# Summing the first norm's squares on TensorE, and loading X and the first weights ahead of parameters and bias rows

## The chip, the cores and the metric

The kernel runs on one core of a Trainium2 chip. The metric is the device time in microseconds (us) of one execution; lower is better. A core has TensorE (matmuls, PE in the profile), VectorE (DVE), ScalarE (ACT), GpSimd (POOL) and SyncE (SP), each with its own instruction queue, and 16 DMA engines that all queues share.

## The reference

A trunk of two layers over X, 1024 tokens of 1024 features in float32. The change touches only the first layer's first norm:

```python
def rmsnorm(x, g):
    xf = x.astype(jnp.float32)
    y = xf * lax.rsqrt(jnp.mean(xf * xf, axis=-1, keepdims=True) + NORM_EPS)
    return (y * g.astype(jnp.float32)).astype(x.dtype)
...
for l in range(DEPTH):
    h = rmsnorm(x, mix_norm_gain[l])
    proj = h @ w_in[l]
...
    x = x + y @ w_out[l]
    x = x + conv_ffn(rmsnorm(x, ffn_norm_gain[l]), ...)
```

`proj` feeds three mixers (an SSD scan, a gated MLP, dilated attention); their concatenated result goes through `w_out`, and a convolutional FFN follows.

## The kernel before

**Layout.** X lies transposed in on-chip memory: 8 tiles (k) of 128 features by 1024 tokens. The tokens are worked in two halves (th = 0, 1) of 512. Every float32 product is made of three matmuls (`mm3`, or the three of `tokens_part`) of a high and a low part: HH and HL for the activations, WH and WL for the weights. GpSimd splits each weight unit, as it arrives in RAW, into WH and WL, two halves a unit; there are two slots, and a unit takes a slot when TensorE has begun the unit after it.

**Engines.** Each engine runs one program, written out by hand and tied to the others by semaphores. Nothing is reordered across waits on an engine. TensorE's first real work is `keys_unit`: for th = 0, then 1, and k = 0 to 7, it waits for h_ready of that k and runs 12 matmuls (four token tiles by three).

**The first norm before.** The squares i = 0 to 7 belong to th = 0, i = 8 to 15 to th = 1.
- ScalarE (`first_norm`, `squares`, line 962) waits for a quarter of X for each four squares and writes the square of one k: the first of each half into ACC, the others into four buffers SQ.
- VectorE (`total`, line 1325) adds each SQ buffer into ACC: 14 adds in all.
- TensorE (`norm_spread`, line 501) sums ACC over the 128 features with 4 small matmuls against a column of ones, once per half, into a PSUM bank (NB).
- VectorE (`mean`, lines 1329 and 1331) makes mean and reciprocal, ScalarE (`root`, line 966) the root, TensorE (`norm_back`, line 509) spreads the result over the partitions.
- For each k VectorE scales X (`scaled`, line 1340, into HF), ScalarE copies HF to HH (`high_norm`, line 972), VectorE subtracts (`low_norm`, line 1346, HL), which raises h_ready.

In `keys_unit` of layer 0 `norm_spread` of the second half stands ahead of k = 5 and `norm_back` ahead of k = 7. VectorE's adds of the second half stand between its tiles of the first.

**Transfers.** SyncE's queue: the constants CST (266 KB; identity, triangles, ones), then X in four quarters of 1 MB, with the first weight unit (two halves of 512 KB) ahead of the third quarter. ScalarE's queue: OH, TAB and ROW (the tables of the relative bias, needed by a small product behind `keys_unit`, line 614), then PARM (layer parameters, 847 KB), which waits for TensorE's first increments; VectorE waits for PARM ahead of the first `mean`.

Of the kernel before, what the change touches and what calls it, by code (L numbers as in the profile page):

```python
# [25 lines left out]
P = 128  # L26
DEPTH, SEQ, DM = 2, 1024, 1024
KT = DM // P
# [11 lines left out]
NG = FFN // UC  # L40
# [61 lines left out]
NB = (3, 7)  # L102
# [31 lines left out]
def trunk(nc, xT, wst, params, consts, onehot, lnrow, table, outT):  # L134
# [10 lines left out]
    with ExitStack() as ctx:  # L145
# [14 lines left out]
        PARM = place("PARM", [P, NPAR])  # L160
        CST = place("CST", [P, 4 * P + 20])
# [25 lines left out]
        TAB = place("TAB", [NBUCK, AH_], top[0])  # L187
        NACS = place("NACS", [P, NT, 16])
        QGN = place("QGN", [P, 1])
        ident, tri_f, tri_b, ones = (CST[:, i * P:(i + 1) * P] for i in range(4))  # L190
# [23 lines left out]
        ACC = place("ACC", [P, SEQ], u_at + 16384)  # L214
        SQ = place("SQ", [P, 4, HALF], u_at + 24576)
        HF = place("HF", [P, 4, HALF], u_at + 32768)
        ROW = place("ROW", [AH_, 2 * SEQ], u_at + 40992)
        OH = place("OH", [NBUCK, 2 * SEQ], u_at + 49184)
# [55 lines left out]
        PS = ctx.enter_context(nc.psum_tensor("PS", [P, 8, HALF], F32))  # L274

        def sem(name):
# [4 lines left out]
        cst_in, par_in, oh_in = sem("cst_in"), sem("par_in"), sem("oh_in")  # L281
# [3 lines left out]
        sq_ready, sq_used, ss_ready = sem("sq_ready"), sem("sq_used"), sem("ss_ready")  # L285
        inv_ready, rs_ready, nb_ready, ib_ready = sem("inv_ready"), sem("rs_ready"), sem("nb_ready"), sem("ib_ready")
# [38 lines left out]
        f_tap, f_conv, f_silu, f_hi, act_ready, f_step = (  # L325
            sem("f_tap"), sem("f_conv"), sem("f_silu"), sem("f_hi"), sem("act_ready"), sem("f_step"))
# [11 lines left out]
        def half(th):  # L338
            return slice(th * HALF, (th + 1) * HALF)
# [23 lines left out]
        def _(sp):  # L363
# [11 lines left out]
                    with sp.Fori(first, last) as u:  # L375
                        unit(u)

            sp.dma_start(CST[:], consts[:, :]).then_inc(cst_in, 16)
            for i in range(4):
                k, th = slice(i % 2 * 4, i % 2 * 4 + 4), i // 2  # L380
                if i == 2:
# [21 lines left out]
            for l in range(DEPTH):  # L403
# [43 lines left out]
                for part in range(2):  # L447
                    sp.wait_ge(yn_ready, l * NT + 6 + 2 * part)
                    sp.wait_ge(yt_full, 2 + l * NT + 6 + 2 * part)
                    k = slice(part * 4, part * 4 + 4)  # L450
# [29 lines left out]
        def _(pe):  # L480
# [15 lines left out]
            def norm_spread(n, th):  # L496

                pe.wait_ge(sq_used, n * SUMS + norm_done(n, th))
                for t in range(4):
                    a = th * HALF + t * P  # L500
                    last = nc.tensor.matmul(PS[:, NB[th], 2 * t:2 * t + 2], ACC[:, a:a + P], ones[:, 0:2],  # L501
                                            start=True, stop=True)
                last.then_inc(nb_ready, 1)

            def norm_back(n, th):

                pe.wait_ge(rs_ready, 2 * n + th + 1)
                for t in range(4):
                    last = nc.tensor.matmul(PS[:, NB[th], t * P:(t + 1) * P],  # L509
                                            IR[:, th, t:t + 1].to_broadcast((P, P)), ident, start=True, stop=True)  # L510
                last.then_inc(ib_ready, 1)
# [61 lines left out]
            def keys_unit(l, a0):  # L573

                n = 2 * l
                unit_ready(l, 0)
                if l:
                    pe.wait_ge(a_free, 4 + a0)
                for th in range(2):
                    for k in range(KT):  # L580
                        if th == 0 and k == (2 if n else 5):
                            norm_spread(n, 1)
                        if th == 0 and k == (5 if n else 7):
                            norm_back(n, 1)
                        pe.wait_ge(h_ready, (2 * n + th) * KT + k + 1)
                        for t in range(th * 4, th * 4 + 4):
                            if k == 0:
                                bank_ready(a0, t)
                            last = tokens_part(0, t, k, A_BANK[t], l > 0 and t == k == 0)
                            if k == KT - 1:  # L590
                                last.then_inc(a_full, 1)
# [11 lines left out]
            for l in range(DEPTH):  # L603
                a0, b0 = l * A_FILLS, l * B_FILLS
                if l == 0:
                    norm_spread(0, 0)
                    norm_back(0, 0)
                keys_unit(l, a0)
                if l == 0:
# [3 lines left out]
                    for q in range(4):  # L613
                        last = nc.tensor.matmul(PS[0:AH_, 4 + q, :], TAB[:, :], OH[:, q * HALF:(q + 1) * HALF],
                                                start=True, stop=True)
# [277 lines left out]
                n = 2 * l + 1  # L893
# [51 lines left out]
        def _(act):  # L945
            A = nc.scalar.activation

            def squares(n, b_value, first, end):

                for i in range(first, end):  # L950
                    dt, th = norm_order(n)[i]
                    if n:
                        act.wait_ge(b_free, b_value + i + 1)
                    else:
                        act.wait_ge(x_in[i // 4], 16)
                    to = ACC[:, half(th)]
                    if i in norm_sums(n):
                        j = norm_sums(n).index(i)
                        if j >= 4:
                            act.wait_ge(sq_used, n * SUMS + j - 3)  # L960
                        to = SQ[:, j % 4, :]
                    A(to, X[:, dt, half(th)], ACT.Square).then_inc(sq_ready, 1)
# [5 lines left out]
            def high_norm(n, th, first, end):  # L968
                for k in range(first, end):
                    i = (2 * n + th) * KT + k  # L970
                    act.wait_ge(hf_ready, i + 1)
                    A(HH[:, k, half(th)], HF[:, i % 4, :], ACT.Copy).then_inc(hh_ready, 1)
# [9 lines left out]
                      ).then_inc(vh_ready, 1)  # L982

            def first_norm():
                squares(0, 0, 0, 8)
                root(0, 0)
                high_norm(0, 0, 0, 4)
                squares(0, 0, 8, 13)
                high_norm(0, 0, 4, 5)
                squares(0, 0, 13, 15)  # L990
                high_norm(0, 0, 5, 6)
                squares(0, 0, 15, 16)
                root(0, 1)
                high_norm(0, 0, 6, KT)
                high_norm(0, 1, 0, 1)
                token_out(0, 0)
                high_norm(0, 1, 1, KT)
# [26 lines left out]
                root(n, 1)  # L1024
                high_norm(n, 1, 0, KT)

            act.dma_start(OH[:], onehot[:, :]).then_inc(oh_in, 16)
            act.dma_start(TAB[:], table[:, :]).then_inc(oh_in, 16)
            act.dma_start(ROW[:], lnrow[:, :]).then_inc(oh_in, 16)
            act.sem_inc(a_free, 4)  # L1030
            for l in range(DEPTH):
                a0, b0 = l * A_FILLS, l * B_FILLS
                act.wait_ge(act_ready, 1 + l * NG * 2)
                act.dma_start(PARM[:], params[l]).then_inc(par_in, 16)
                nc.scalar.preload_act_table(ACT.Sqrt)
                if l == 0:
                    first_norm()
# [153 lines left out]
                for i in range(NT):  # L1191
                    n, par = l * NT + i, i % 2
# [4 lines left out]
                    if i == 2:  # L1197
# [3 lines left out]
                        for h in range(4):  # L1201
                            last = A(MHL[:, :, h, :], PS[:, 6, 0:2 * P].rearrange("p (a n) -> p a n", a=2), ACT.Copy,
                                     scale=fourth[:, h:h + 1])
# [26 lines left out]
                for c in range(NT):  # L1230
                    n, par = l * NT + c, c % 2
# [7 lines left out]
                    for j in range(4):  # L1239
# [4 lines left out]
                        for h in range(4):  # L1244
                            e = d * 8 + g * 4 + h
                            last = A(SEG[par][:, j, h, :], PS[:, 2 + j % 2, h * P:(h + 1) * P], ACT.Exp,
                                     bias=NACS[:, c, e:e + 1])
# [5 lines left out]
                    for h in range(HEADS):  # L1253
                        cols = slice(h * HD, (h + 1) * HD)
                        last = A(Y2[:, cols], PS[:, 6, cols], ACT.Copy, scale=EACS[:, c, 8 + h:9 + h])
# [17 lines left out]
                for g in range(NG):  # L1273
                    n = l * NG + g
# [40 lines left out]
        def _(dve):  # L1315
            TT, STT, TS = nc.vector.tensor_tensor, nc.vector.scalar_tensor_tensor, nc.vector.tensor_scalar

            def total(n, i):

                th = norm_order(n)[i][1]  # L1320
                j = norm_sums(n).index(i)
                dve.wait_ge(sq_ready, n * 16 + i + 1)
                if j:
                    dve.wait_ge(sq_used, n * SUMS + j)
                TT(ACC[:, half(th)], ACC[:, half(th)], SQ[:, j % 4, :], ALU.add).then_inc(sq_used, 1)  # L1325
# [23 lines left out]
            def scale_on(n, th, first, end):  # L1349

                for k in range(first, end):
                    if k < KT:
                        scaled(n, th, k)
                    if k:
                        low_norm(n, th, k - 1)

            def first_norm():
                for i in range(1, 8):
                    total(0, i)
                dve.wait_ge(par_in, 16)  # L1360
                mean(0, 0)
                scale_on(0, 0, 0, 4)
                for i in range(9, 12):
                    total(0, i)
                scale_on(0, 0, 4, 5)
                for i in range(12, 14):
                    total(0, i)
                scale_on(0, 0, 5, 6)
                for i in range(14, 16):
                    total(0, i)  # L1370
                mean(0, 1)
                scale_on(0, 0, 6, KT + 1)
                scale_on(0, 1, 0, KT + 1)

            def mix_norm(n, add):
# [50 lines left out]
            for l in range(DEPTH):  # L1426
# [56 lines left out]
                for x in range(2):  # L1483
                    nc.vector.memset(PAD[:, x, 0:2], 0.0)
                    last = nc.vector.memset(PAD[:, x, SEQ + 2:SEQ + 4], 0.0)
# [451 lines left out]
```

## Time and profile before

| | |
|---|---|
| median of 3 runs | 2678.39 us (2677.86 to 2683.78) |
| the profiled execution | 2681.2 us, of it 2679.4 us span |
| TensorE busy | 2575.6 us (96%) |
| VectorE / ScalarE / GpSimd busy | 1482.6 / 896.7 / 730.8 us |
| mean granted TensorE clock | 0.988 of full |

Times in the trace count from the span's start. PE is TensorE's matmuls, PEld its weight loads, which overlap; a float32 matmul of tiles that are not split shows as two entries. PEclk is the granted clock as a share of 2.4 GHz. In a timeline row the bracket says how long the engine was idle before the instruction, and what released it.

### The profile page before, as it was taken

The page shows a single profiled execution, that of the slowest core. Times are in us where ns is not written, and L with a number is a line of the kernel's source. Part 1 is how long each engine was busy: PE and PEld are TensorE (multiplying, and loading weights), DVE is VectorE, ACT ScalarE, POOL GpSimd, SP SyncE. Part 2 cuts the span into 40 slices and gives each one's busy share as a digit, 9 for nine tenths or more (in the row PEclk, how much of TensorE's full clock was granted, in tenths as well). Part 3 has the DMA queues.
Part 4 walks back from the last instruction along what each step waited for, and adds up shares of the span by engine and source line. Part 5 has one row for each costly group of instructions (what it writes and reads, how often), then busy time and mean ns, then how long its engine had stood idle before and what let it go on. Part 6 is the DMA issues. An engine that isn't in the chain of part 4 may idle for free. (4 is left out here: it accounts for less than half of the span.)

```text
span 2679.4 us, 33472 instructions
## 1 busy us (share of the span) xinstructions
PE 2575.6 (96%) x13350; PEld 2177.3 (81%) x13350; DVE 1482.6 (55%) x1743; ACT 896.7 (33%) x1550; POOL 730.8 (27%) x388
## 2 busy tenths in 40 slices
PE   5999998899999999999999999988999999999998
PEld 5988986788888888888789889877888888888887
DVE  5376558837444444444575755696464444444445
ACT  3245556613222222222233465574132222222221
POOL 2332111024333333333323311100433333333331
PEclk8999999899999999999999999999999999999999
DMA  4443443121111111111123344521111111111111
GB/s 177 144 117 119 132 152 124 48 81 48 47 47 48 48 53 48 49 47 48 54 109 80 109 134 140 171 85 69 48 47 48 47 47 48 49 51 50 48 47 71
DMA packets 73725, 209.90 MB, mean 78 GB/s; under 512 B 5832, under 2 KB 28360, under 8 KB 72264
## 3 DMA queue, kind: packets, MB, share of 16 engines
q1 hardware_dynamic: 53384, 178.58, 20.3%
q10 hardware_dynamic: 20200, 29.30, 3.3%
q8 instruction: 106, 1.74, 0.3%
q14 instruction: 35, 0.29, 0.0%
HBM read 176.37 MB, written 31.49 MB: 78 GB/s over the span
## 5 line engine op out<-in xcount | busy, mean ns | idle before, releaser
L484 PE MATMUL PS<-HH,WH 128*128 128x512 f32 x1920 | 756.6, 394 | 4.9 <-issue 4.9
L474 POOL CAST WH<-RAW 128x1024 fp32r<-128x1024 f32 x192 | 238.7, 1243 | 1888.3 <-PE PS L484 1403.2
L488 PE MATMUL PS<-HH,WL 128*128 128x512 f32 x1920 | 753.3, 392 | 0.0
L487 PE MATMUL PS<-HL,WH 128*128 128x512 f32 x1920 | 753.2, 392 | 0.0
L476 POOL TENSOR_TENSOR WL<-RAW,WH 128x1024 fp32r<-128x1024 f32 x192 | 497.4, 2591 | 15.4
L1755 DVE TENSOR_TENSOR X<-PS,X 128x512 f32<-128x512 f32 x384 | 259.6, 689 | 378.7 <-PE PS L488 378.4
L484 PEld LDWEIGHTS PS<-HH,WH 128*128 128x128 f32 x1920 | 362.5, 189 | 84.3 <-issue 5.3
L488 PEld LDWEIGHTS PS<-HH,WL 128*128 128x128 f32 x1920 | 361.7, 188 | 81.3
L487 PEld LDWEIGHTS PS<-HL,WH 128*128 128x128 f32 x1920 | 362.2, 189 | 78.3
L1284 ACT ACTIVATE FPAD<-PS 128x512 f32<-128x512 f32 x176 | 102.6, 596 | 885.8 <-PE PS L488 885.8
L1773 DVE SCALAR_TENSOR_TENSOR CVV<-FPAD,PARM,CVV 128x1024 f32<-128x1024 f32 x44 | 95.3, 2166 | 377.8 <-ACT CVV L1290 377.8
L484 PE MATMUL PS<-AHI,WH 128*128 128x512 f32 x704 | 278.9, 396 | 4.9 <-DVE X L1755 4.9
L488 PE MATMUL PS<-AHI,WL 128*128 128x512 f32 x704 | 278.5, 396 | 0.0
L487 PE MATMUL PS<-ALO,WH 128*128 128x512 f32 x704 | 278.0, 395 | 0.0
L555 PE MATMUL PS<-WH,HH 128*128 128x256 f32 (+1 forms) x896 | 264.4, 295 | 12.7 <-DVE HL L1346 12.7
L558 PE MATMUL PS<-WL,HH 128*128 128x256 f32 (+1 forms) x896 | 256.9, 287 | 0.0
L559 PE MATMUL PS<-WH,HL 128*128 128x256 f32 (+1 forms) x896 | 256.9, 287 | 0.0
L555 PEld LDWEIGHTS PS<-WH,HH 128*128 128x128 f32 x896 | 174.1, 194 | 16.5 <-DVE HL L1346 9.0
L558 PEld LDWEIGHTS PS<-WL,HH 128*128 128x128 f32 x896 | 174.2, 194 | 0.1
L559 PEld LDWEIGHTS PS<-WH,HL 128*128 128x128 f32 x896 | 174.0, 194 | 0.0
L484 PEld LDWEIGHTS PS<-AHI,WH 128*128 128x128 f32 x704 | 133.1, 189 | 37.0 <-DVE X L1755 6.6
L488 PEld LDWEIGHTS PS<-AHI,WL 128*128 128x128 f32 x704 | 132.9, 189 | 31.3
(198 smaller groups left out, 3080.9 us busy)
## 6 DMA issues: line engine op xcount, KB each, us to landing
RAW<-wst SPq DMA_DIRECT2D x192, 512.0 KB, 3.5
TOE<-toe_d SPq DMA_DIRECT2D x64, 512.0 KB, 3.7
XBS<-xbc_d SPq DMA_DIRECT2D x24, 512.0 KB, 4.5
xspill<-X ACTq DMA_DIRECT2D x2, 4096.0 KB, 13.1
xbc_d<-CV ACTq DMA_DIRECT2D x16, 512.0 KB, 3.9
X<-xspill SPq DMA_DIRECT2D x4, 2048.0 KB, 7.3
tok_d<-ST ACTq DMA_DIRECT2D x12, 512.0 KB, 3.4
ZG<-tok_d SPq DMA_DIRECT2D x16, 384.0 KB, 3.6
```

Source lines behind the costliest of these rows:

```text
L474: nc.gpsimd.tensor_copy(hi, raw).then_inc(hi_done, 1)
L476: nc.gpsimd.tensor_tensor(lo, raw, hi.bitcast(F32), ALU.subtract).then_inc(w_ready, 1)
L484: ins = nc.tensor.matmul(out, wh, xh, start=first, stop=False)
L487: nc.tensor.matmul(out, wh, xl, start=False, stop=False)
L488: return nc.tensor.matmul(out, wl, xh, start=False, stop=last)
L555: ins = nc.tensor.matmul(o, xh, wh, start=(k == 0), stop=False)
L558: nc.tensor.matmul(o, xh, wl, start=False, stop=False)
L559: return nc.tensor.matmul(o, xl, wh, start=False, stop=(k == KT - 1))
L1284: A(FPAD[:, x % 2, 1 + th * HALF:1 + (th + 1) * HALF], bank(f % 4), ACT.Copy).then_inc(a_free, 1)
L1755: TT(x, bank(4 + i % 4), x, ALU.add).then_inc(b_free, 1)
L1773: step.then(STT(t, FPAD[:, x % 2, 0:SEQ], PARM[:, at:at + 1], t, ALU.mult, ALU.add))
```

## The change

- `first_norm` on VectorE loses all 14 `total`. In their place TensorE gets `square_sum(i)`: for each of the 16 squares, four matmuls of the kind of `norm_spread`, accumulated over k in the bank. Squares 0 to 7 are summed ahead of `norm_back(0, 0)`; squares 8 to 15 in pairs ahead of k = 1 to 4 of `keys_unit`. The `norm_spread` of both halves goes from the first norm. TensorE frees the SQ buffers.
- ScalarE's squares of the second half go in pairs between its copies of k = 0 to 3.
- CST moves from SyncE's queue to the front of ScalarE's. PARM of layer 0 is issued behind square 3, without a wait for TensorE, and OH, TAB and ROW behind square 7.

```diff
@@ sync
-            sp.dma_start(CST[:], consts[:, :]).then_inc(cst_in, 16)
             for i in range(4):
@@ tensor
+            def square_sum(i):
+
+                th, k = divmod(i, KT)
+                pe.wait_ge(sq_ready, i + 1)
+                square = SQ[:, (th * (KT - 1) + k - 1) % 4, :] if k else ACC[:, half(th)]
+                for t in range(4):
+                    last = nc.tensor.matmul(PS[:, NB[th], 2 * t:2 * t + 2], square[:, t * P:(t + 1) * P], ones[:, 0:2],
+                                            start=(k == t == 0), stop=(k == KT - 1), skip_group_check=True)
+                if k:
+                    last.then_inc(sq_used, 1)
+                if k == KT - 1:
+                    pe.wait_ge(sq_used, (th + 1) * (KT - 1))
+                    pe.sem_inc(nb_ready, 1)
@@ keys_unit
-                        if th == 0 and k == (2 if n else 5):
+                        if th == 0 and n and k == 2:
                             norm_spread(n, 1)
+                        if th == 0 and not n and 1 <= k < 5:
+                            square_sum(6 + 2 * k)
+                            square_sum(7 + 2 * k)
                         if th == 0 and k == (5 if n else 7):
                             norm_back(n, 1)
@@ layer 0
-                    norm_spread(0, 0)
+                    for i in range(KT):
+                        square_sum(i)
                     norm_back(0, 0)
@@ scalar, first_norm
-                squares(0, 0, 0, 8)
+                squares(0, 0, 0, 4)
+                act.dma_start(PARM[:], params[0]).then_inc(par_in, 16)
+                squares(0, 0, 4, 8)
+                act.dma_start(OH[:], onehot[:, :]).then_inc(oh_in, 16)
+                act.dma_start(TAB[:], table[:, :]).then_inc(oh_in, 16)
+                act.dma_start(ROW[:], lnrow[:, :]).then_inc(oh_in, 16)
                 root(0, 0)
-                high_norm(0, 0, 0, 4)
-                squares(0, 0, 8, 13)
-                high_norm(0, 0, 4, 5)
-                squares(0, 0, 13, 15)
-                high_norm(0, 0, 5, 6)
-                squares(0, 0, 15, 16)
+                for k in range(4):
+                    high_norm(0, 0, k, k + 1)
+                    squares(0, 0, 8 + 2 * k, 10 + 2 * k)
+                high_norm(0, 0, 4, 6)
                 root(0, 1)
@@ scalar, ahead of the layers
-            act.dma_start(OH[:], onehot[:, :]).then_inc(oh_in, 16)
-            act.dma_start(TAB[:], table[:, :]).then_inc(oh_in, 16)
-            act.dma_start(ROW[:], lnrow[:, :]).then_inc(oh_in, 16)
+            act.dma_start(CST[:], consts[:, :]).then_inc(cst_in, 16)
...
-                act.wait_ge(act_ready, 1 + l * NG * 2)
-                act.dma_start(PARM[:], params[l]).then_inc(par_in, 16)
+                if l:
+                    act.wait_ge(act_ready, 1 + l * NG * 2)
+                    act.dma_start(PARM[:], params[l]).then_inc(par_in, 16)
@@ vector, first_norm
-                for i in range(1, 8):
-                    total(0, i)
                 dve.wait_ge(par_in, 16)
                 mean(0, 0)
-                scale_on(0, 0, 0, 4)
-                for i in range(9, 12):
-                    total(0, i)
-                scale_on(0, 0, 4, 5)
-                for i in range(12, 14):
-                    total(0, i)
-                scale_on(0, 0, 5, 6)
-                for i in range(14, 16):
-                    total(0, i)
+                scale_on(0, 0, 0, 7)
                 mean(0, 1)
-                scale_on(0, 0, 6, KT + 1)
+                scale_on(0, 0, 7, KT + 1)
```

## Rows read from the trace of the kernel before

**Rows 1.** The page: the engines' shares, and the chain's engines.

```profile
PE 2575.6 (96%) x13350; PEld 2177.3 (81%) x13350; DVE 1482.6 (55%) x1743; ACT 896.7 (33%) x1550; POOL 730.8 (27%) x388
...
PE 30%; DVE 1%; issue 0%; ACT 0%; DVEq 0%
```

**Rows 2.** Waits of TensorE, whole span: us in total, times, longest.

```profile
PE PS L501 <- DVE ACC L1325: 21.9, 5, 17.3
...
PE PS L555 <- DVE HL L1346: 12.7, 8, 3.4
```

**Rows 3.** Timeline to 25 us, all engines: start, duration, engine and line.

```profile
6.67 0.36 ACTq L1034 DMA_DIRECT2D PARM<-par  x1
...
9.22 0.63 ACT L962 ACTIVATE ACC<-X 128x512 f32<-128x512 f32 x1 [0.87 <-DMA X<-xT]
...
12.91 2.19 ACT L962 ACTIVATE SQ<-X 128x512 f32<-128x512 f32 x4 [1.50 <-DMA X<-xT]
...
15.36 1.39 POOL L474 CAST WH<-RAW 128x1024 fp32r<-128x1024 f32 x1 [14.91 <-DMA RAW<-wst]
...
17.35 1.87 PE L501 MATMUL PS<-CST,ACC 128*128 128x2 f32 x8 [17.35 <-DVE ACC L1325]
...
19.99 2.07 PE L509 MATMUL PS<-CST,IR 128*128 128x128 f32 x8 [0.78 <-ACT IR L966]
...
22.10 1.40 DVE L1340 SCALAR_TENSOR_TENSOR HF<-X,PARM,PS 128x512 f32<-128x512 f32 x2 [2.40 <-PE PS L509]
...
25.00 0.55 PE L555 MATMUL PS<-WH,HH 128*128 128x256 f32 x1 [2.94 <-DVE HL L1346]
```

**Rows 4.** Transfers issued before 130 us: KB each, us to landing.

```profile
PARM<-par ACTq DMA_DIRECT2D x1, 847.0 KB, 7.9
...
OH<-onehot ACTq DMA_DIRECT2D x1, 256.0 KB
```

**Rows 5.** One microsecond by engine; last two columns DMA share and GB/s.

```profile
9.00:10.00 1.00, 0.00 (x0) 0.00 (x0) 0.00 (x0) 0.78 (x2) 0.00 (x0) 1.00 1.06 391
```

**Rows 6.** Line 501 alone in a stretch: PE busy, PEld busy, PEclk, DMA, GB/s.

```profile
590.00:600.00 10.00, 0.95 (x8) 1.05 (x8) 1.00 0.00 1
```

**Rows 7.** Timeline from 28 to 49 us, POOL's last row and TensorE's.

```profile
28.61 2.73 POOL L476 TENSOR_TENSOR WL<-RAW,WH 128x1024 fp32r<-128x1024 f32 x1
...
34.80 0.39 PE L555 MATMUL PS<-WH,HH 128*128 128x256 f32 x1 [3.37 <-DVE HL L1346]
...
40.19 1.70 PE L501 MATMUL PS<-CST,ACC 128*128 128x2 f32 x8
...
44.61 0.41 PE L558 MATMUL PS<-WL,HH 128*128 128x256 f32 x1
...
47.17 0.41 PE L558 MATMUL PS<-WL,HH 128*128 128x256 f32 x1
...
48.88 1.43 PE L509 MATMUL PS<-CST,IR 128*128 128x128 f32 x8
...
54.08 0.28 PE L555 MATMUL PS<-WH,HH 128*128 128x256 f32 x1
...
55.50 0.28 PE L555 MATMUL PS<-WH,HH 128*128 128x256 f32 x1
```

**Rows 8.** VectorE's lines before 64 us: count, busy us, mean ns, idle before.

```profile
L1325 DVE TENSOR_TENSOR ACC<-ACC,SQ 128x512 f32<-128x512 f32 x14 | 11.5, 821 | 13.2 <-ACT SQ L962 12.2
```

**Rows 9.** Busy us (count) of PE, PEld, DVE, ACT, POOL; PEclk, DMA, GB/s.

```profile
29.20:36.00 6.80, 3.43 (x29) 3.22 (x29) 5.65 (x7) 4.04 (x8) 2.14 (x1) 1.00 0.33 128
36.02:43.50 7.48, 5.14 (x24) 4.76 (x23) 4.22 (x10) 1.89 (x4) 0.00 (x0) 0.50 0.01 2
43.50:49.60 6.10, 6.01 (x28) 6.01 (x29) 1.99 (x4) 0.73 (x2) 0.00 (x0) 0.50 0.01 1
...
64.10:66.70 2.60, 2.04 (x6) 0.43 (x6) 0.00 (x0) 2.35 (x3) 0.00 (x0) 1.00 1.10 463
66.80:69.50 2.70, 2.70 (x4) 0.25 (x2) 0.00 (x0) 0.00 (x0) 0.00 (x0) 0.50 0.90 388
```

## The prediction

> **What bounds the kernel now.** I read the page first: TensorE is busy for 96% of the span, and the chain that ended last is TensorE's wherever the profile can follow it [rows 1]. So a microsecond saved elsewhere is worth nothing unless TensorE starts earlier or waits less. The waits of TensorE come next: its longest is the first one, 17.3 us until the first ACC, and line 555 waits 12.7 us in all for HL, 3.4 us at the most [rows 2]. These are what this edit can reach. The timeline to 25 us shows the opening in its order: squares from 9.22 as X lands, spread at 17.35 to 19.22, norm_back at 19.99, the first scaled tile at 22.10, the first product at 25.00 [rows 3]. Behind it TensorE has only its own program, and nothing later is ahead of it by itself: what it loses or gains before the end of the keys' unit it loses or gains at the end. Last I read the opening's clock. The same 12 matmuls of one k take 2.56 us from 44.61 to 47.17 and 1.42 us from 54.08 to 55.50 [rows 7]. Those are the two levels, 1.2 and 2.4 GHz.
>
> **Part 1: sums on TensorE in place of VectorE's adds, first half of the tokens.** Removed: VectorE's chain of 7 adds and one spread. A spread is four matmuls (8 entries), each with a 128x128 weight load for 2 columns. It takes 1.70 us at half clock (at 40.19 [rows 7]) and 0.95 us at full [rows 6]. A square_sum is this same spread for one square, so eight of them stand where one stood. The squares come every 0.55 us, the sums take 1.71 us each: TensorE is then the slower end, and the squares wait for it.
> - X comes earlier. PARM (847 KB), OH (256 KB) and ROW leave the front, CST only changes its queue. At 391 KB a microsecond [rows 5] OH and ROW, 0.29 MB, are worth 0.7 us before X's first quarter; the bounds are 0 and 1.4. PARM was issued at 6.67 and lay across X's second quarter, but squares 4 to 7, finished at 15.1 [rows 3], are needed only at 9 + 4 x 1.71 = 15.8 us, so that this part of the reorder pays nothing. I take X at 8.4, and the first square done at 8.4 + 0.63 = 9.0.
> - Eight sums at half clock: 9.0 + 8 x 1.71 = 22.7, with the last result 22.85. Before it was 19.22 (17.35 + 1.87).
> - PARM is issued after square 3, near 10.5, and took 7.9 us to land [rows 4]: 18.5, before 22.85. It is covered by the sums; without that cover it would set the mean.
> - From the spread's end to the first scaled tile it was 2.88 us, from there to the first product 2.90 [rows 3]. Both stay: GpSimd's weight work still runs then (to 31.34 before [rows 7], a microsecond earlier at most after), and slows the HL subtractions.
> Sum: the first product at 28.6 in place of 25.0, **+3.6 us**, bounds +2.9 (HL without GpSimd beside it) and +4.4 (X no earlier).
>
> **Part 2: the other eight sums, between products.** Before, from the first product (25.00) to norm_back of the second half (48.88) went 23.9 us: waits for VectorE's adds (3.37 us at 34.80 alone [rows 7]), a spread, and 7 groups of 12 products. After, VectorE has lost 14 adds of 0.82 us [rows 8], 11.5 us, and can deliver a k every 1.4 us (0.70 for a scaled tile [rows 3] and, by my estimate, as much for its subtraction); TensorE no longer waits for it, but carries 8 sums more. All at half clock: 7 x 2.56 + 8 x 1.71 = 31.6 us. The last three groups are unbroken; the unbroken stretch from 43.50 ran at half for 6.1 us and then at full [rows 7, 9], so the rise falls into them and gives back about 1.3: 30.3, or **+6.4 us**. With full clock from the second group on: 2.56 + 6 x 1.42 + 8 x 0.95 = 18.7, or -5.2.
> Which of the two? In 36.02 to 43.50 TensorE was busy 5.14 of 7.48 us with products and one spread and stayed at half. In 64.10 to 69.50 it was busy with the small table's matmuls nearly throughout, and the clock fell and stayed low [rows 9]. So busy time in itself doesn't hold it, and a group of 2.56 us behind 3.4 us of 2-column sums looks like the first of these. Against it, 29.20 to 36.00 had TensorE busy for half of the time and kept full clock: once up, products at 1.42 in every 3.3 us might keep it up for some groups. I give the low side four parts in five: 6.4 - 0.2 x 11.6 = **+4.1 us**.
>
> The second half of the tokens has no sums and no fewer waits: norm_back at k = 7, then a k each 1.4 us, as before: 0. The squares on ScalarE (1.1 us for two [rows 3]) and a copy, about one square long, fit into the 3.3 to 6 us that TensorE takes for a k. Four SQ buffers, now freed by TensorE, hold squares 13 to 15 back until sums 9 to 11 are done, and the HH copies of k = 3 to 5 behind them; these stand a group ahead of their use, so this costs nothing, but up to 2 us if a group slipped. OH, TAB and ROW, issued after square 7, are wanted behind the keys' unit, at 64.10 [rows 9] or later, some 50 us on. PARM for layer 0 no longer waits for TensorE's first increments, nor does the table load.
>
> Total: 3.6 + 4.1 = +7.7 us. The profiled execution took 2681.2 us (span 2679.4 and 1.8 around it), which gives 2688.9. It is 2.8 us above the median of the runs shown, 2678.39, so for the median I say **2686.1 us**.
>
> The Trainium skill, "TensorE: Matmul & The Clock Gate", in the section on why this matters for kernels, asks to keep TensorE busy continuously for the full clock; its Part 1 ties the clock to how busy the engine has been. By it 14 us of unbroken sums would raise the clock before the first product, and the sum would be some 7 us below the old time and not above. The stretch at 64.10 [rows 9] speaks against taking busy time as the measure. It is the third rival.
>
> **Rivals.**
> - Partly full clock (the same time within 0.2%, 5.4 us, which is about what a measurement can tell): one low group more or less is worth 2.56 + 3.42 - 3.32 = 2.7 us. If the clock rises behind the second or third group and holds, part 2 gives 0 to -2.5 and the total is +1 to +4: 2681. For it speaks 29.20 to 36.00; against it 36.02 to 43.50.
> - All low and more: waits between the sums (each waits for its own square) at 0.1 us each, X no earlier: 3.6 + 0.8 + 6.4 + 1.5 = +12.3, 2690.7. The runs of before span 6 us, so such shifts exist.
> - The opposite sign: the unbroken sums raise the clock. Three at half (9.0 to 14.1) and five at 0.95 end at 18.9; norm_back takes 1 us less; the first product comes at 24.2, held by GpSimd's second half of the weights, -0.8. Then 7 x 1.42 + 7.6 = 17.5 for 23.9, -6.4. Total -7.2: 2671.2. It decides from the point where full clock is there by about 26 us and stays; a rise only after the first product gives at best 3.6 - 5.2 = -1.6, no longer a gain that can be told. Against it: the half clock after the spread and norm_back at 17.35 to 22.06, and 64.10 to 69.50.
> - The reorder does nothing: X is not earlier; inside the range, +0.7 on the forecast.
>
> **How the numbers follow.** Mostly low clock, with the worse variant: 0.62. Partly full: 0.25. Opposite sign: 0.13. The range has to take the first two and the bounds of part 1: 2677 (partly full with X at its best) to 2693 (all low, waits, late X). Slower by over 0.2% (above 2683.7) 0.62, within 0.2% 0.26, faster 0.12.
>
> **What would show it.** Right: 64 entries of matmuls with 2 columns before the first mean, PE busy from 9 to 23 us without a gap, the first product near 28.6 us, granted clock 0.50 through most of 29 to 56 us, norm_back of the second half near 57, TensorE's waits for HL almost gone, the end of the keys' unit near 72 in place of 64.1, and from there the same distances as before. Wrong: sums spaced at 0.12 per entry before 20 us, which is the third rival; the first product before 26 us; products of k = 1 to 4 at 1.42 us a group; or a new wait of line 555 for HL, which would say that the HH copies behind the squares are late. If the sums cost much less than the spread does, both parts shrink together and the change turns to a gain of the adds that it removes.

## The result, and the profile after

The changed kernel is slower: a median of 2684.74 us (2675.80 to 2693.56, 22 executions) against 2677.75 us (2671.73 to 2683.78, 22), a ratio of 1.0027 with a 95% interval of 1.0018 to 1.0036, or about +7.2 us. The forecast was 2686.1. Two things are to be seen at once: the loss, and that the single times are now 18 us apart where they were 12. The profiled execution took 2676.36 us (span 2674.6), one of the fastest of its kernel, so its trace shows the good case and not the median. The profiled execution of the kernel before (2681.2 us) lies on the slow side of its own kernel. Compared with each other, the two traces hide the loss.

The page, TensorE's share and the chain's engines, which answer to [rows 1]:

```profile
PE 2585.0 (97%) x13462; PEld 2189.0 (82%) x13462; DVE 1471.5 (55%) x1729; ACT 896.5 (34%) x1550; POOL 729.2 (27%) x388
...
PE 30%; DVE 1%; issue 0%; ACT 0%; DVEq 0%
```

TensorE is busy 9.4 us more, and is the bound as before. The timeline of the changed kernel to 34 us, all engines, as [rows 3] and [rows 7] (line 510 is the sum, 522 norm_back, 568 the first of a product's three matmuls):

```profile
6.70 0.63 ACT L979 ACTIVATE ACC<-X 128x512 f32<-128x512 f32 x1 [4.12 <-DMA X<-xT]
...
7.40 1.84 PE L510 MATMUL PS<-CST,ACC 128*128 128x2 f32 x8 [7.40 <-ACT ACC L979]
...
9.11 12.09 PE L510 MATMUL PS<-CST,SQ 128*128 128x2 f32 x56
...
10.82 1.04 POOL L473 CAST WH<-RAW 128x1024 fp32r<-128x1024 f32 x1 [10.38 <-DMA RAW<-wst]
...
21.40 0.16 DVE L1348 TENSOR_SCALAR MS<-PS 128x4 f32<-128x4 f32 x1 [21.40 <-PEq L516]
...
22.07 2.08 PE L522 MATMUL PS<-CST,IR 128*128 128x128 f32 x8 [0.87 <-ACT IR L983]
...
24.18 1.40 DVE L1359 SCALAR_TENSOR_TENSOR HF<-X,PARM,PS 128x512 f32<-128x512 f32 x2 [2.41 <-PE PS L522]
...
27.53 0.55 PE L568 MATMUL PS<-WH,HH 128*128 128x256 f32 x1 [3.39 <-DVE HL L1365]
...
30.23 1.17 PE L510 MATMUL PS<-CST,ACC 128*128 128x2 f32 x8
...
31.25 1.03 PE L510 MATMUL PS<-CST,SQ 128*128 128x2 f32 x8
...
33.65 1.84 PE L510 MATMUL PS<-CST,SQ 128*128 128x2 f32 x16
```

The first square comes at 6.70 us (9.22 before) and the first weight cast at 10.82 (15.36), so the loads did move. Behind them stand 64 entries of line 510: the first 8 begin at 7.40, and the other 56 take 12.09 us without a break. That is 0.216 an entry, as in the spread of eight entries at half clock in [rows 7] (1.70 us). The mean comes at 21.40 (19.32 before), the first scaled tile at 24.18 (22.10), the first product at 27.53 (25.00). Then comes the first pair of sums, still partly at half clock (1.17 us); from 31.25 on eight entries take 1.03 and sixteen 1.84. In this execution the clock rose behind the first group of products. The columns PEclk of the stage tables print 1.00 in the opening before the first recorded change of the clock, so that the spacing of the rows is the thing to read there.

X's first quarter came 2.5 us earlier. The rows of one microsecond each, with DMA share and GB/s in the last two columns, show more than the bytes that left the queues. The first two are of the kernel before, the third of the changed one:

```profile
3.00:4.00 1.00, 0.00 (x0) 0.00 (x0) 0.00 (x0) 0.00 (x0) 0.00 (x0) 1.00 0.89 217
4.00:5.00 1.00, 0.00 (x0) 0.00 (x0) 0.00 (x0) 0.00 (x0) 0.00 (x0) 1.00 1.03 183
...
4.00:5.00 1.00, 0.00 (x0) 0.00 (x0) 0.00 (x0) 0.00 (x0) 0.00 (x0) 1.00 1.03 391
```

With the old order the engines were about as busy and moved half as much: 200 GB/s from 3 to 5 us before, and 380 in the changed kernel. The experiments agree: 233 in sums only, which has the old order, 371 in loads only. Which of the transfers made it slow isn't shown.

The second norm_back of the same trace, against 48.88 in [rows 7]:

```profile
46.37 1.05 PE L522 MATMUL PS<-CST,IR 128*128 128x128 f32 x8
```

From first product to here it is 18.8 us (23.9 before). The waits of TensorE up to 64 us (us in total, times, longest) against [rows 2]:

```profile
PE PS L510 <- ACT ACC L979: 7.4, 1, 7.4
PE PS L568 <- DVE HL L1365: 4.2, 2, 3.4
```

The first wait fell from 17.3 to 7.4 us and line 568's before HL to 4.2, all but 0.8 of it the wait for the first one. TensorE no longer waits; it works instead.

### The profile page after: what moved, and what is told of

Its sections match the earlier page's. It is cut to its first block and busy times, and to the rows that moved or that the text cites. A ratio compares the mean times of both kernels' runs of the same rounds, so it can differ in the third digit from the quotient of the medians.

```text
span 2674.6 us, 33671 instructions
## 1 busy us (share of the span) xinstructions
PE 2585.0 (97%) x13462; PEld 2189.0 (82%) x13462; DVE 1471.5 (55%) x1729; ACT 896.5 (34%) x1550; POOL 729.2 (27%) x388
```

## The experiments

Each ratio is to executions of the kernel before on the same chip, with a 95% interval. Where single traces are compared, the stretches are "first product" (its start from the span's start) and "products" (from there to the second norm_back). For the kernel before they are 25.0 and 23.9 us.

A trace is one execution, and the part behind the opening varies whatever the edit: from the start of the small product behind `keys_unit` (64.68 us in the trace before) to the end of the span, the twelve kept traces take between 2610.3 and 2619.9 us. So a trace shows the order and the clock of the opening; what an edit costs is read from the ratios.

**The changed kernel again**, unchanged.

> The changed kernel once more, unchanged, for a second profile. The first profiled execution (2676.36 us) was one of the fastest of its 22 runs, and its clock rose at 30.7 us, behind the first group of products. Theory A (the stage of products and 2-column sums runs at half clock in the slow executions and at full in the fast ones): an execution near the median or above shows 0.50 through the sums between products, and its time above 2676 is the longer first product to norm_back stretch: 18.8 us in the fast one, up to 30 here. Theory F (the spread of times arises later in the program): the same 19 us stretch and a longer rest.

One execution, 2681.89 us. Its stage table for two stretches (us and entries of PE, PEld, DVE, ACT, POOL, then PEclk, DMA share, GB/s):

```profile
28.00:36.00 8.00, 8.00 (x39) 8.00 (x39) 5.05 (x7) 3.59 (x7) 3.24 (x2) 1.00 0.41 133
36.60:44.00 7.40, 7.40 (x67) 7.40 (x67) 1.95 (x3) 2.30 (x4) 0.00 (x0) 1.00 0.00 0
```

39 entries in 8 us until 36 (0.205 each, the half clock), 67 in 7.4 behind it (0.110). The clock rose one group of products later than in the first trace. First product 27.72 (27.53), products 21.5 us (18.8). Those 2.7 us are about half of the 5.5 us between the two times; the rest lies behind the keys' unit, where the clock falls in other places from one execution to the next (from 1360 to 1380 us it is 1.00 on average in the first trace and 0.91 here). So both theories have a part in the spread.

**Split: the same sums, one of each pair moved into the middle of the products.**

```diff
 if th == 0 and not n and 1 <= k < 5:
     square_sum(6 + 2 * k)
-    square_sum(7 + 2 * k)
...
 for t in range(th * 4, th * 4 + 4):
+    if not n and t == 2 and 1 <= k < 5:
+        square_sum(7 + 2 * k)
```

> The changed kernel, but of each pair of sums ahead of k = 1 to 4 the second stands in the middle of that k's 12 products, so that no more than six products of that stage stand together. Same instructions, same count. Theory A (an unbroken group of 12 products, 2.56 us at half clock, is what raised the clock in the fast executions, at 30.7 and 36.5 us; which group does it is chance): now the clock stays at 0.50 until after the sums in every execution; first product to norm_back 29 to 31 us instead of 18.8 and 21.5; median near 2689, ratio 1.0045, and the times are less spread than the changed kernel's 2676 to 2693. Rival (place does not matter, the sums cost their time): ratio 1.0027 as before.

Measured: ratio 1.0047 (1.0034 to 1.0061), 2687.23 to 2693.29 us in 6 executions, median 2689.15. The sums in TensorE's timeline, and the stage table:

```profile
30.80 1.70 PE L510 MATMUL PS<-CST,ACC 128*128 128x2 f32 x8
...
33.78 1.70 PE L510 MATMUL PS<-CST,SQ 128*128 128x2 f32 x8
...
51.70 1.70 PE L510 MATMUL PS<-CST,SQ 128*128 128x2 f32 x8
```

```profile
28.10:36.00 7.90, 7.90 (x37) 7.90 (x38) 4.56 (x5) 2.73 (x6) 2.09 (x1) 1.00 0.34 119
36.00:46.00 10.00, 10.00 (x49) 10.00 (x49) 3.30 (x5) 3.03 (x6) 0.00 (x0) 1.00 0.00 0
46.00:56.80 10.80, 10.65 (x50) 10.59 (x51) 2.27 (x5) 1.27 (x3) 0.00 (x0) 1.00 0.01 2
56.90:60.00 3.10, 3.10 (x29) 3.10 (x29) 0.28 (x1) 0.00 (x0) 0.00 (x0) 1.00 0.00 0
```

Eight sums of 1.70 us, one each 2.99 us (51.70 is the last), and TensorE busy for 28.55 of the 28.7 us from 28.1 to 56.8, all at half clock: 49 entries in 10 us (PEclk prints 1.00 here too, before the first recorded change). Directly behind the sums and some unbroken products it is 29 entries in 3.1 us. The products stretch is 30.5 us (28.10 to 58.63). The number of instructions is that of the changed kernel; only the place differs, and the median is 4.4 us above the changed kernel's. The rival's 1.0027 lies below the interval, but the changed kernel's own interval reaches 1.0036, and nine of its 22 times are above 2689 us. The clean comparison is the next one, on the same chip. The times are less spread, as expected: 6 us against 18.

**Bunched: all eight sums of the second half ahead of k = 1.**

```diff
-if th == 0 and not n and 1 <= k < 5:
-    square_sum(6 + 2 * k)
-    square_sum(7 + 2 * k)
+if th == 0 and not n and k == 1:
+    for i in range(8, 16):
+        square_sum(i)
```

> The changed kernel with all eight sums of the second half together ahead of k = 1, so that the products of k = 1 to 6 stand together. Theory A: the sums cost 8 x 1.71 at half clock in most executions (8 x 0.95 where the clock has risen behind k = 0), the clock rises within 4 to 6 us behind them: first product to norm_back about 27 us, median near 2685, ratio 1.0027, below the split kernel by 3 to 5 us. Rival (place does not matter): the same time as split.

Ratio 1.0022 (1.0011 to 1.0034), median 2684.78 us. The sums and norm_back in TensorE's timeline:

```profile
30.69 1.70 PE L510 MATMUL PS<-CST,ACC 128*128 128x2 f32 x8
32.25 12.09 PE L510 MATMUL PS<-CST,SQ 128*128 128x2 f32 x56
...
55.55 1.05 PE L522 MATMUL PS<-CST,IR 128*128 128x128 f32 x8
```

64 entries at half clock again (1.70 and 12.09 us); products 27.5 us (28.00 to 55.55), of which 13.7 are sums. It lies 4.4 us below split by the medians, as theory A has it, and beside the changed kernel. Both ran on one chip: all six times of split are above 2687 us, ten of bunched's twelve below. So the rival, that place doesn't matter, is out. The trace shown is the slowest of the twelve executions, and in it too the clock rose only behind the last sum.

**Wide: each sum against 128 columns of ones in place of 2.** One result column in 128 is read.

```diff
-last = nc.tensor.matmul(PS[:, NB[th], 2 * t:2 * t + 2], square[:, t * P:(t + 1) * P], ones[:, 0:2],
+last = nc.tensor.matmul(PS[:, NB[th], t * P:(t + 1) * P], square[:, t * P:(t + 1) * P], ones,
...
-TS(MS[:, th], PS[:, NB[th], 0:8:2], 1.0 / DM, ...
+TS(MS[:, th], PS[:, NB[th], slice(0, 8, 2) if n else slice(0, HALF, P)], 1.0 / DM, ...
```

> The changed kernel, with each sum against 128 columns of ones in place of 2, so that its results fill a bank (one column in 128 is read). The count of matmuls and weight loads is the same, and a 128x128 matmul takes no longer than the weight load beside it (norm_back: 8 in 1.05 us at full clock, the spread 0.95). Theory A (the clock falls or stays low because sums with 2 columns do not hold it up): granted clock rises during the first eight sums, the first product near 24 us, the stage of products and sums all at full clock; total 6 to 7 us below the kernel before, ratio 0.9976, and a spread of times no wider than before's. Theory E (the sums cost what they cost by their number, whatever their columns): ratio 1.0027 as the changed kernel, or a little more.

Ratio 0.9978 (0.9968 to 0.9987), median 2672.73 us, nine of ten executions between 2669.2 and 2673.2; the profiled one is the tenth, 2678.43. TensorE's timeline:

```profile
8.54 2.05 PE L510 MATMUL PS<-CST,ACC 128*128 128x128 f32 x8 [8.54 <-ACT SQ L979]
10.38 7.89 PE L510 MATMUL PS<-CST,SQ 128*128 128x128 f32 x56
19.15 1.16 PE L522 MATMUL PS<-CST,IR 128*128 128x128 f32 x8 [0.87 <-ACT IR L983]
22.62 0.36 PE L568 MATMUL PS<-WH,HH 128*128 128x256 f32 x1 [2.32 <-DVE HL L1365]
...
24.45 1.91 PE L510 MATMUL PS<-CST,ACC 128*128 128x128 f32 x8
26.16 1.52 PE L510 MATMUL PS<-CST,SQ 128*128 128x128 f32 x8
...
28.93 1.95 PE L510 MATMUL PS<-CST,SQ 128*128 128x128 f32 x16
...
41.73 1.05 PE L522 MATMUL PS<-CST,IR 128*128 128x128 f32 x8
```

Two stretches of the same trace (columns as above):

```profile
7.00:13.00 6.00, 4.46 (x21) 4.49 (x22) 0.00 (x0) 3.25 (x6) 1.94 (x2) 1.00 1.04 414
13.50:18.40 4.90, 4.77 (x43) 4.58 (x41) 0.00 (x0) 1.26 (x2) 4.31 (x3) 1.00 1.05 388
```

The first eight entries take 2.05 us (1.84 with two columns); the next 56 take 7.89 in place of 12.09. The clock rose among them, near 13 us: 0.212 us an entry until then, 0.111 behind it. In wide and its variant below, the 56 take 7.89 and 7.63 us. In all six kept traces with two columns that have them (the two of the changed kernel, split, bunched, half 1, sums only) they take 12.09, so chance from one execution to the next hardly explains it. norm_back comes at 19.15 (22.07 in the changed kernel), the first product at 22.62, and products take 19.1 us (22.62 to 41.73). Between norm_back and the first product TensorE idled, and the sums at 24.45 and 26.16 run slow once more; from 28.93 on all is at full clock. Fuller matmuls, 64 times as many columns, made the kernel about 12 us faster than the changed one by the medians, 13 by the two ratios, and faster than the kernel before. Theory E is out.

**Wide, with 12 idle matmuls behind the first norm_back** (their results are overwritten).

```diff
 norm_back(0, 0)
+for i in range(12):
+    nc.tensor.matmul(PS[:, NB[1], 0:P], ident, ones, start=True, stop=True)
```

> The wide version with 12 idle 128-column matmuls of constants behind the first norm_back, where TensorE waited 2.3 us for the first HL and the clock fell to 0.50 from 23.5 to 26.9 us (their result is overwritten). Theory A (it is the clock): full clock from the first sums on, 1.5 to 2 us below the wide version, ratio 0.9971. Rival (the clock falls there anyway, or VectorE's subtractions beside GpSimd set that stretch): the ratio of the wide version, 0.9978.

Ratio 0.9975 (0.9965 to 0.9985), median 2670.38 us, against 2676.26 of the kernel before on its chip. Line 626 is the filling:

```profile
19.96 2.84 PE L626 MATMUL PS<-CST 128*128 128x128 f32 x24
...
24.07 1.05 PE L510 MATMUL PS<-CST,ACC 128*128 128x128 f32 x8
...
40.14 1.05 PE L522 MATMUL PS<-CST,IR 128*128 128x128 f32 x8
```

The pair of sums behind the first products now runs at full clock (1.05 us), and products take 17.6 us in place of 19.1. The trace has the 1.5 us that were expected; the intervals of the two ratios overlap almost wholly, so the measurement doesn't tell the two kernels apart. The rival isn't excluded by the times; that the clock fell there anyway is excluded by the trace. Both beat the kernel before.

**Loads only: the new order of transfers, all adds on VectorE.**

```diff
-sp.dma_start(CST[:], consts[:, :]).then_inc(cst_in, 16)
...
+act.dma_start(CST[:], consts[:, :]).then_inc(cst_in, 16)
...
-squares(0, 0, 0, 8)
+squares(0, 0, 0, 4)
+act.dma_start(PARM[:], params[0]).then_inc(par_in, 16)
+squares(0, 0, 4, 8)
+act.dma_start(OH[:], onehot[:, :]).then_inc(oh_in, 16)
...
```

> The transfer order of the changed kernel alone; all sums and adds as before. The changed kernel's trace has the first square at 6.70 us (before 9.22) and GpSimd's first weight cast at 10.82 (before 15.36). Theory A (the loads are a gain that the sums on TensorE hide): without the sums, VectorE's chain ends near 15.5 instead of 19.2, the first product comes near 21 us, the total is 3 to 4.5 us below the kernel before, ratio 0.9985. Theory B (as the prediction had it, squares do not gain more than 0.7 us from the loads): ratio 0.9997, no change. If the second half of the parameters' transfer now sets the mean, the first product stays near 25 us.

Ratio 1.0001 (0.9992 to 1.0010): nothing. My theory A fell, and theory B's number held without its reason. The timeline shows why:

```profile
6.99 0.63 ACT L961 ACTIVATE ACC<-X 128x512 f32<-128x512 f32 x1 [4.41 <-DMA X<-xT]
...
8.17 8.73 DVE L1328 TENSOR_TENSOR ACC<-ACC,SQ 128x512 f32<-128x512 f32 x7 [8.17 <-ACT SQ L961]
...
11.13 1.04 POOL L473 CAST WH<-RAW 128x1024 fp32r<-128x1024 f32 x1 [10.68 <-DMA RAW<-wst]
...
16.95 1.87 PE L500 MATMUL PS<-CST,ACC 128*128 128x2 f32 x8 [16.95 <-DVE ACC L1328]
...
24.00 0.55 PE L554 MATMUL PS<-WH,HH 128*128 128x256 f32 x1 [2.32 <-DVE HL L1349]
```

The first square is 2.2 us earlier than before, yet the spread begins at 16.95, only 0.4 earlier. VectorE's seven adds stretch over 8.73 us, and in the middle GpSimd starts to split weights, at 11.13 in place of 15.36. VectorE's line for these adds (count, busy us, mean ns, idle before), first in the kernel before, then here:

```profile
L1325 DVE TENSOR_TENSOR ACC<-ACC,SQ 128x512 f32<-128x512 f32 x7 | 5.5, 784 | 11.8 <-ACT SQ L962 11.3
...
L1328 DVE TENSOR_TENSOR ACC<-ACC,SQ 128x512 f32<-128x512 f32 x7 | 8.1, 1157 | 8.8 <-ACT SQ L961 8.2
```

784 ns was its mean in this window before, and 1157 now. Within the trace too: until GpSimd starts at 11.13 nearly four of the adds have 2.64 us busy, and the rest takes 5.46. The earlier weights took back most of what the earlier X gave. The first product still comes at 24.00, a microsecond earlier than in the trace before; the ratio doesn't show it.

**Late weights: loads only, with the first weight unit behind all of X.**

```diff
 for i in range(4):
     k, th = slice(i % 2 * 4, i % 2 * 4 + 4), i // 2
-    if i == 2:
-        weights(0, 0, 1)
     sp.dma_start(X[:, k, half(th)], xT[:, k, half(th)]).then_inc(x_in[i], 16)
+weights(0, 0, 1)
```

> The loads alone, but with the first weight unit behind all of X, so that GpSimd starts near 16 to 17 us. Theory H (in the loads-only version VectorE's seven adds took 8.7 us from 8.17 to 16.90 because GpSimd split weights beside them): the adds of the first half end near 13 us, the spread near 15, and the first mean is 3 to 4 us earlier than with the loads alone. Rival (the adds wait for squares or the parameters): they end near 16.9 as before.

One execution, 2674.05 us. VectorE's adds, and TensorE's longest waits up to 60 us:

```profile
L1327 DVE TENSOR_TENSOR ACC<-ACC,SQ 128x512 f32<-128x512 f32 x7 | 4.8, 692 | 8.9 <-ACT SQ L960 8.3
```

```profile
PE PS L499 <- DVE ACC L1327: 13.8, 1, 13.8
PE PS L553 <- POOL WL L474: 10.7, 1, 10.7
```

Without GpSimd beside them the adds take 692 ns each, and the spread begins at 13.78, 3.2 us earlier than with the loads alone: theory H holds. But GpSimd's first cast comes at 21.14, later than the expected 16 to 17, and TensorE waits 10.7 us for WL: the first product comes at 29.18. That needn't cost the kernel anything: products then take 17.4 us, and the second norm_back comes at 46.60 (46.10 in loads only). One time, inside the range of the kernel before, says nothing of the whole. What is shown is that, with the adds on VectorE, early weights slow the chain that early X starts.

**Half 1: TensorE sums only the first half's squares; new loads.**

In addition to the edit of loads only:

```diff
-norm_spread(0, 0)
+for i in range(KT):
+    square_sum(i)
...
-for i in range(1, 8):
-    total(0, i)
```

> New loads, and TensorE sums only the first half's eight squares; the second half is added by VectorE as before. Theory A (both halves cost): first product near 27.5 us as in the changed kernel, waits for the adds between products as before, total +2.5 us on the kernel before, ratio 1.0009. Theory C (the loss is all in the second half's sums between products): ratio below 1.0000.

Ratio 1.0011 (1.0002 to 1.0020), as expected; first product 28.14 us:

```profile
28.14 0.55 PE L568 MATMUL PS<-WH,HH 128*128 128x256 f32 x1 [2.68 <-DVE HL L1364]
```

**Half 2: TensorE sums only the second half's; new loads.**

In addition to the edit of loads only:

```diff
-if th == 0 and k == (2 if n else 5):
+if th == 0 and n and k == 2:
     norm_spread(n, 1)
+if th == 0 and not n and 1 <= k < 5:
+    square_sum(6 + 2 * k)
+    square_sum(7 + 2 * k)
...
```

VectorE's adds of the second half go, and ScalarE's squares stand as in the changed kernel.

> New loads, the first half added by VectorE, TensorE sums the second half's squares in pairs between products. Theory A: first product near 21 us (-4), then on the mean of low and high clock +4.5 us, total within 1.5 us of the kernel before, ratio 1.0000 to 1.0005, with a spread of single times as wide as the changed kernel's (some 15 us). Theory D (the loss is all in the first half): ratio 0.9985 and a narrow spread of times.

Ratio 1.0015 (1.0004 to 1.0026), 2675.14 to 2689.75 us. The spread is wide, as expected, but the level is 3 to 4 us higher than expected: the first product was to come near 21.

```profile
24.86 0.55 PE L568 MATMUL PS<-WH,HH 128*128 128x256 f32 x1 [3.11 <-DVE HL L1364]
```

It came at 24.86, since here too VectorE's adds stand beside GpSimd's work. Its products stretch was 28.6 us in the profiled execution (norm_back at 53.42). The pairs of sums stand as in the changed kernel, but here the second and third took 3.41 us for 16 entries and only the last 1.91: the clock rose behind the fourth group of products. By the ratio it is +4.0 us with the first product where it was, so this is the direct measure of part 2.

**Sums only: all sums on TensorE, transfers as before.**

> All sums on TensorE with 2 columns, transfers as before. Theory A (in the version with sums the early X is worth its whole 2.5 us, because TensorE starts summing when X lands): total 2.5 us above the changed kernel, +9.5 us on the kernel before, ratio 1.0035. Theory G (the loads are worth nothing here either, as alone): ratio 1.0027.

Ratio 1.0041 (1.0029 to 1.0053), 6 executions; first product 30.61 us, 2.9 and 3.1 behind the changed kernel's two traces:

```profile
30.61 0.55 PE L569 MATMUL PS<-WH,HH 128*128 128x256 f32 x1 [4.25 <-DVE HL L1362]
```

That is theory A's 2.5 us or a little more; theory G's ratio lies just outside the interval. The new loads are worth about 0.0014, or 3.7 us, in the version with sums (the intervals of the two ratios overlap, so the size is rough), and nothing in the version with adds.

## Why the prediction was right

- **The sign and the size.** +7.7 us was forecast, about +7.2 measured; 2686.1 against 2684.74. The forecast stood on the median of the three executions known then, 0.6 us above that of the 22. Half 1 (+2.9 us) and half 2 (+4.0) together give +6.9, with intervals of 0.5 to 5.4 and 1.1 to 7.0, so each part has about the size that was forecast, and no part is known to better than 2 or 3 us.
- **Part 1, +3.6 us.** The first product came 2.5 us later in the first trace and 2.7 to 3.1 later in those of the same opening (after_again, half1, split, bunched). Half 1 gives +2.9 us by its ratio. The number of sums and 1.71 us for each were right. PARM was issued at 6.71 and not near 10.5, since the issue didn't wait for the squares; it was covered either way. X was mis-sized: its first square came 2.5 us earlier and not 0.8. The prediction divided the bytes that left by 391 GB/s, but in the old order the engines moved only 217 and 183 in the microseconds from 3 and 4. Of the 2.5 us, the four traces lose 1.2 again at norm_back (23.2 to 23.4 us, 22.07 in the first trace), because TensorE's first sum begins near 8.6 us though the first square is done at 7.6. The constants had landed by then, 4.4 to 4.6 us after their issue at 0.74. In sums only, with the old order, there is no such gap (first square done at 9.54, first sum at 9.59). What holds it with the new order no run settles. So a gain that was too small and a loss that wasn't foreseen partly cancel in the +3.6.
- **Part 2, +4.1 us.** The two ends were -5.2 (full clock from the second group on) and +6.4 (half clock throughout). The first trace is the one end, 18.8 us for the 18.7 worked out; split is the other, 30.5 us for 30.3. The median lies between, at the remaining 7.2 - 2.8 = 4.4, and half 2 measures +4.0. The ends were arithmetic from the rows. That four parts in five lean to the low end was a choice, and that it hit is in part luck: both kept traces of the changed kernel are faster than its median, and how many of the 22 executions ran low no trace shows. The 23.9 us that it was set against are one execution too, at 0.50 from 36.02 to 49.6 [rows 9], 3.5 us slower than its kernel's median; in loads only, with the same adds and a ratio of 1.0001, the stretch was 22.1 us.
- **The clock.** The argument was that TensorE, though busy with the sums, would stay at half clock. It did, in six traces of six. Wide changes only the width of the sums: same place, same count, fuller matmuls, and the clock rises among the first sums, in two traces of two. Split shows the other side: 28 us of a busy TensorE at half clock. What the prediction had only as an estimate, that the rise between the sums is chance, is shown by the first trace of the changed kernel against its second, and by half 2, where it rose later still. That the place of the sums decides is shown by split and bunched, which differ in nothing else. Why is less certain. The expectation was that unbroken groups of products raise the clock; with the groups broken up the rise came only behind the last sum, but so it did in the one trace of bunched.
- **The rival of the opposite sign** was right about its consequence and wrong about its condition. If the opening sums raised the clock the kernel was to take 2671.2 us; wide, in which they do, takes 2672.7 (by the ratios -5.9 us, for the -7.2 of the rival). The Trainium skill, "TensorE: Matmul & The Clock Gate", section "Why this matters for your kernels", asks to keep TensorE busy continuously. Split's 28.55 busy us out of 28.7 at half clock don't agree with that: busy as the profile counts it, and half clock all the same.
- **The loads.** The prediction gave the new order 0.7 us for X and nothing for the rest. In the changed kernel it is worth more (about 3.7 us, roughly), and alone it is worth nothing that the ratio shows; that GpSimd's earlier weight split would slow VectorE's adds was not in the prediction, and in the changed kernel it doesn't matter because those adds are gone. That is the one real merit of the change: it frees VectorE to let X and the weights come early. Wide keeps the merit and pays for it less.
- **Not right:** a granted clock of 0.50 from 29 to 56 us as the thing to see. It is what split shows; the two traces of the changed kernel had it only until about 30.7 and 36.5 us. With it went the rest of that list: norm_back near 57 (46.37 and 49.18) and the end of the keys' unit near 72 (the small product behind it starts at 61.79 and 64.59). Groups of products at full clock from k = 1 on, which the first trace has, stood among the signs of being wrong. One trace of a kernel whose executions differ this much could not have told right from wrong; the 22 times and the split into halves did.

What stays open: why TensorE's first sum waits until 8.6 us in most traces, which transfer slowed the old order, and what decides behind which group the clock rises.

## What to carry to other kernels

Moving sums to an idle TensorE is free only until its own work could start. Here eight sums took 13.8 us at half clock, longer than the chain of adds they replaced, and put the first product back. If TensorE has to do filler-like work ahead of or between its real products, give each matmul many columns: here 128 took no longer than 2 (eight entries at full clock in 1.05 us and 1.03), and it turned a loss of 0.27% into a gain of 0.22%. Where small matmuls must be issued amid real products, try them in one block, or between whole groups of products, before breaking the groups up. And before a transfer is moved forward, ask which engine it wakes up: here it woke GpSimd beside VectorE's adds, and the gain was gone.

## What the runs showed of the hardware that was not expected

- A busy TensorE stayed at half clock for 28.7 us, with two-column matmuls between its products (split).
- VectorE's 128x512 additions in on-chip memory took 692 ns on average alone (late weights) and 1157 ns where most of them ran beside GpSimd's casts and subtractions (loads only).
- 56 entries of sums took 12.09 us with 2 columns, and 7.89 us with 128: the fuller ones were the faster, because the clock rose among them.
- With the same busy share of the DMA engines (0.96 and 1.02), 3 to 5 us into the kernel, the old order of transfers moved 200 GB/s and the new one 380.
